# A mixer's output projection split into two passes over token halves, with the norms behind it overlapped

## The reference, cut to what matters

```python
def second_block(...):
    for l in range(DEPTH_2):                       # one layer
        mix = hybrid_mixer(rmsnorm(h, norm_mix_pre[l]), w_in[l], w_ret_out[l], w_sb_out[l], w_out[l])
        h = h + rmsnorm(mix, norm_mix_post[l])
        ff = swiglu(rmsnorm(h, norm_ffn_pre[l]), w_ffn_in[l], w_ffn_out[l])
        h = h + rmsnorm(ff, norm_ffn_post[l])
    return h[:, N_META:]

def hybrid_mixer(...):
    ...
    merged = jax.nn.sigmoid(ga) * y_ret + jax.nn.sigmoid(gb) * y_sb
    return merged @ w_out                          # the projection that is split

def rmsnorm(x, g):
    y = x * rsqrt(mean(x * x, axis=-1) + 1e-6)     # mean over the 1024 features of a token
    return y * g

def swiglu(hn, w_ffn_in, w_ffn_out):
    a, b = split(hn @ w_ffn_in, 2)
    return (silu(a) * b) @ w_ffn_out
```

## Time and profile before

| what | value |
|---|---|
| time of 3 runs, median | 2991.72 us (2991.7 to 2993.84) |
| the profiled execution | 2994.3 us, of which the profile spans 2992.6 |
| TensorE matmul busy | 2905.2 us (97%), 17931 matmuls |
| VectorE / ScalarE / GpSimd busy | 1464.2 / 1101.7 / 211.3 us |
| share of the chain that ended last | PE 62%, DVE 4%, ACT 1% |
| DMA | 225.63 MB, mean 75 GB/s |
| a weight load of 512 KB, issue to landing | 3.7 to 4.1 us (3.4 for 448 KB) |

### The profile page before, as it was taken

The page is one execution under the profiler, slowest core; times in us unless marked ns, Lnnn a source line. Parts: engine busy times, 40 slices in busy tenths (PEclk is TensorE's granted clock), DMA queues, the critical chain, the costliest instruction groups (busy, mean ns, idle before and its releaser), DMA issues.

```text
span 2992.6 us, 46575 instructions
## 1 busy us (share of the span) xinstructions
PE 2905.2 (97%) x17931; PEld 2517.2 (84%) x17931; DVE 1464.2 (49%) x2102; ACT 1101.7 (37%) x1763; POOL 211.3 (7%) x177
## 2 busy tenths in 40 slices
PE   8999999999989999799999999999999999799998
PEld 7878879999989999799988888888888887588887
DVE  5555545555347776555543454453433335544422
ACT  4333334333235554333322223223344444332322
POOL 1000001000011221100001011011000000200000
PEclk9999989999999999899999999999999999899999
DMA  4222213332331111133333322322311112133332
GB/s 126 55 53 60 62 30 92 91 90 85 91 105 57 49 56 44 53 94 91 91 91 99 95 67 87 89 68 74 88 45 54 42 54 78 58 98 95 92 91 73
DMA packets 419559, 225.63 MB, mean 75 GB/s; under 512 B 7589, under 2 KB 416422, under 8 KB 419350
## 3 DMA queue, kind: packets, MB, share of 16 engines
q1 hardware_dynamic: 416438, 211.45, 24.4%
q0 software_dynamic: 2256, 10.32, 1.2%
q10 hardware_dynamic: 784, 2.75, 0.3%
HBM read 222.36 MB, written 2.13 MB: 75 GB/s over the span
## 4 chain that ended last, share of the span: by engine, by line
PE 62%; DVE 4%; issue 2%; ACT 1%; POOL 0%; DVEq 0%; ACTq 0%; POOLq 0%
PE ps L436 33%; PE ps L440 17%; PE ps L1038 2%; PE ps L854 2%; PE ps L996 1%; PE ps L1059 1%; PE ps L1027 1%; DVE wl L403 1%; PE ps L963 1%; PE ps L899 1%; PE ps L1031 0%; DVE rl L2143 0%; DVE xl L470 0%; DVE post_t L518 0%; DVE h L521 0%
## 5 line engine op out<-in xcount | busy, mean ns | idle before, releaser
L403 DVE TENSOR_TENSOR wl<-raw,wh 128x1024 fp32r<-128x1024 f32 (+4 forms) x429 | 518.8, 1209 | 401.6 <-ACT wh L399 398.0
L399 ACT ACTIVATE wh<-raw 128x1024 fp32r<-128x1024 f32 (+4 forms) x429 | 428.5, 999 | 729.7 <-PE ps L436 394.1
L440 PE MATMUL ps<-xh,wh 128*128 128x264 f32 x2736 | 571.4, 290 | 14.4 <-DVE xl L470 5.5
L440 PE MATMUL ps<-xl,wh 128*128 128x264 f32 x2736 | 559.4, 286 | 0.0
L440 PE MATMUL ps<-xh,wl 128*128 128x264 f32 x2736 | 559.1, 286 | 0.0
L440 PEld LDWEIGHTS ps<-xh,wh 128*128 128x128 f32 x2736 | 429.6, 190 | 24.3 <-issue 7.4
L440 PEld LDWEIGHTS ps<-xl,wh 128*128 128x128 f32 x2736 | 427.2, 189 | 0.0
L440 PEld LDWEIGHTS ps<-xh,wl 128*128 128x128 f32 x2736 | 425.9, 190 | 0.0
L436 PE MATMUL ps<-xh,wh 128*128 128x512 f32 x976 | 391.6, 401 | 17.7 <-DVE xl L470 14.0
L436 PE MATMUL ps<-xl,wh 128*128 128x512 f32 x976 | 387.8, 397 | 0.0
L436 PE MATMUL ps<-xh,wl 128*128 128x512 f32 x976 | 385.6, 395 | 0.0
(11 more groups left out here) (309 smaller groups left out, 4011.4 us busy)
## 6 DMA issues: line engine op xcount, KB each, us to landing
raw<-in_w_in SPq DMA_DIRECT2D x88, 512.0 KB, 4.0
raw<-in_ffn_w_gate SPq DMA_DIRECT2D x44, 512.0 KB, 3.8
raw<-in_ffn_w_up SPq DMA_DIRECT2D x44, 512.0 KB, 3.8
raw<-in_w_ffn_in SPq DMA_DIRECT2D x44, 512.0 KB, 3.8
raw<-in_fox_w_in SPq DMA_DIRECT2D x33, 512.0 KB, 4.1
raw<-in_hgrn_w_in SPq DMA_DIRECT2D x32, 512.0 KB, 3.9
raw<-in_ffn_w_down SPq DMA_DIRECT2D x32, 448.0 KB, 3.4
raw<-in_ffn_w_down SPq DMA_DIRECT2D x16, 512.0 KB, 3.7
```

What stands on the lines that cost most here:

```text
L399: nc.scalar.activation(wh[:, v % 2, 0:nk, :], raw[:, v % RAW_SLOTS, 0:nk, :], ACT.Copy).then_inc(s("w_hi"), 1)
L403: nc.vector.tensor_tensor(wl[:, v % 2, 0:nk, :], raw[:, v % RAW_SLOTS, 0:nk, :], wh[:, v % 2, 0:nk, :].bitcast(F32), ALU.subtract).then_in ...
L440: last = nc.tensor.matmul(ps[:, bank + b, 0:HALF], w[:, slot, kk, :], x[:, k0 + k, b * HALF:(b + 1) * HALF], start=first, stop=end_)
```

## The change

PH_OUT now makes 256 tokens only (HALF_A), in 8 groups of 24 matmuls of 256 columns; a new phase PH_OUTB does the other 256 (HALF_B) with the same weights, which are loaded and split a second time. Norm, residual and xh, xl of the first half are placed in the steps of the second pass; of tiles 6 and 7 behind it. The first two groups of PH_UP2 are taken together: both over the first 256 tokens, then step by step over the second 256 as its norm goes on. Sums, rstd and squares are done in halves (SQUARES is the order of the squares). Elsewhere some semaphores are merged (p_inv and gate_one to fox_step, h_kept and ff_kept to kept, h_turned and ff_turned to turned), with the same instructions waiting for the same things.

```diff
-PH_UP2 = Phase(PH_OUT, FT // 2, K8, narrow=range(4))
+PH_OUTB = Phase(PH_OUT, 2, K8, narrow=range(4))
+PH_UP2 = Phase(PH_OUTB, FT // 2, K8, narrow=range(4))
...
+HALF_A, HALF_B = (0, SEQ // 2), (SEQ // 2, SEQ)
+SQUARES = [("mix", HALF_A, m) for m in range(KT)] + [("mix", HALF_B, 0), ("mix", HALF_B, 1)]
+for _m in range(2, KT):
+    SQUARES += [("h", HALF_A, _m - 2), ("mix", HALF_B, _m)]
+SQUARES += [("h", HALF_A, KT - 2), ("h", HALF_A, KT - 1)] + [("h", HALF_B, m) for m in range(KT)]
...
-    def post_norm(dve, src, post_row, r, n0, name, rx, next_row):
+    def post_norm(dve, part, m, r, n):
+        t0, t1 = META + part[0], META + part[1]
         dve.wait_ge(s("rstd_ready"), r + 1)
...                                               # post_t, h over t0:t1, as before
+        if m:
+            dve_x(dve, 5 + n // KT, m - 1, ROW_FFNPRE, t0, t1)
...
+        dense(PH_OUTB, dram["w_out_2"][0], 0)
...
TensorE:
-        dense(PH_OUT, mh, ml, ("m_ready", 0))
-        pe_sum(pe, 5, META)
-        dense(PH_UP2, xh, xl, ("x_ready", KT * 5), 6, META)
+        for m in range(KT):
+            pe_group(pe, PH_OUT, m // 4, m % 4, mh, ml, None if m else ("m_ready", 0), tokens=HALF_A)
+        for m in range(KT):
+            pe_group(pe, PH_OUTB, m // 4, m % 4, mh, ml, tokens=HALF_B)
+            if m == 0:
+                half_sum("mix", HALF_A).then_inc(s("ssum"), 1)
...
+        for gj in range(2):
+            pe.wait_ge(s("psum_free"), PH_UP2.g0 + gj + 1)
+            pe.wait_ge(s("w_split"), unit(PH_UP2, 0, gj) + RAW_SLOTS + 1)
+            for k in range(KT):
+                if gj == 0:
+                    pe.wait_ge(s("x_ready"), KT * 5 + k + 1)
+                up_step(gj, HALF_A, k)
+            if gj == 0:
+                half_sum("mix", HALF_B).then_inc(s("ssum"), 1)
+        for k in range(KT):
+            pe.wait_ge(s("x_ready"), KT * 6 + k + 1)
+            for gj in range(2):
+                last = up_step(gj, HALF_B, k)
+                if k == KT - 1:
+                    last.then_inc(s("mm_done"), 1)
+        half_sum("h", HALF_A)
+        half_sum("h", HALF_B).then_inc(s("ssum"), 1)
+        for gj in range(2, 4):
+            pe_group(pe, PH_UP2, 0, gj, xh, xl)
...
ScalarE:
+        for m in range(KT):
+            split_ahead(act, act_hi, PH_OUT, m // 4, m % 4)
+            if m == 4:
+                tables_for(act, "ln_exp")
+            act.wait_ge(s("psum_free"), evacuated(PH_OUT, m // 4, m % 4))
+            half_square("mix", HALF_A, m)
+        for m in range(KT):
+            split_ahead(act, act_hi, PH_OUTB, m // 4, m % 4)
+            if m >= 2:
+                half_x(HALF_A, m - 2)
+            act.wait_ge(s("psum_free"), evacuated(PH_OUTB, m // 4, m % 4))
+            half_square("mix", HALF_B, m)
+            if m == 0:
+                half_rstd(HALF_A, 5)
+        split_ahead(act, act_hi, PH_UP2, 0, 0)
+        half_x(HALF_A, KT - 2)
+        half_x(HALF_A, KT - 1)
+        half_rstd(HALF_B, 6)
+        for m in range(KT):
+            half_x(HALF_B, m)
+        up(2, PH_UP2, 7)
...
VectorE:
+        for m in range(KT):
+            mixed(PH_OUT, m, HALF_A)
+        for m in range(KT):
+            mixed(PH_OUTB, m, HALF_B)
+            if m >= 2:
+                post_norm(dve, HALF_A, m - 2, 5, m - 2)
+        split_ahead(dve, dve_lo, PH_UP2, 0, 0)
+        for m in range(KT - 2, KT):
+            post_norm(dve, HALF_A, m, 5, m)
+        dve_x(dve, 5, KT - 1, ROW_FFNPRE, META, META + HALF_A[1])
+        for m in range(KT):
+            post_norm(dve, HALF_B, m, 6, KT + m)
+        dve_x(dve, 6, KT - 1, ROW_FFNPRE, META + HALF_B[0], L)
+        up(2, PH_UP2, 7)
```

More of the change, by code:

```diff
@@ L413, in group_end, with pe_group @@
         return 2 + unit(ph, i, sum(map(len, ph.groups[:gj + 1])))
-    def pe_group(pe, ph, i, gj, hi, lo, ready=None, k0=0, part=None):
+    def pe_group(pe, ph, i, gj, hi, lo, ready=None, k0=0, part=None, tokens=(0, SEQ)):
         bank = ph.banks[(ph.g0 + gj) % 2]
@@ L435, in pe_group @@
                     if gj in ph.narrow:
-                        last = nc.tensor.matmul(ps[:, bank, 0:SEQ], w[:, slot, kk, :], x[:, k0 + k, META:L],
+                        last = nc.tensor.matmul(ps[:, bank, tokens[0]:tokens[1]], w[:, slot, kk, :],
+                                                x[:, k0 + k, META + tokens[0]:META + tokens[1]],
                                                 start=first, stop=end_)
@@ L511, in dve_add_h @@
         nc.vector.tensor_tensor(hm, hm, out_of(ph, mm), ALU.add).then_inc(s("psum_free"), 1)
-    def post_norm(dve, src, post_row, r, n0, name, rx, next_row):
+    def post_norm(dve, part, m, r, n):
+        t0, t1 = META + part[0], META + part[1]
         dve.wait_ge(s("rstd_ready"), r + 1)
[L516 to L524, removed]
+        nc.vector.scalar_tensor_tensor(post_t[:, m % 2, t0:t1], mix[:, m, t0:t1], col(gains, ROW_MIXPOST + m),
+                                       rstd[:, t0:t1], ALU.mult, ALU.mult).then_inc(s("post_scaled"), 1)
+        dve.wait_ge(s("post_scaled"), n + 1)
+        nc.vector.tensor_tensor(h[:, m, t0:t1], h[:, m, t0:t1], post_t[:, m % 2, t0:t1], ALU.add)\
+            .then_inc(s("h_post"), 1)
+        if m:
+            dve_x(dve, 5 + n // KT, m - 1, ROW_FFNPRE, t0, t1)
     def hgrn_level(n):
@@ L1099, in _, with half_sum, up_step, up_body @@
         dense(PH_SBOUT, oh, ol, ("sb_o_done", 1))
-        dense(PH_OUT, mh, ml, ("m_ready", 0))
-        pe_sum(pe, 5, META)
-        dense(PH_UP2, xh, xl, ("x_ready", KT * 5), 6, META)
+        def half_sum(what, part):
+            t0, t1 = META + part[0], META + part[1]
+            pe.wait_ge(s("sq_used"), square_index(what, part, KT - 1) + 3)
+            return nc.tensor.matmul(ps[:, 4, part[0]:part[1]], mean_d, ssq[:, t0:t1], start=True, stop=True)
+        for m in range(KT):
[4 more added lines that the diff above has]
+                half_sum("mix", HALF_A).then_inc(s("ssum"), 1)
+        def up_step(gj, part, k):
+            bank, slot = PH_UP2.banks[(PH_UP2.g0 + gj) % 2], (PH_UP2.u0 + gj) % 2
+            for n, (w, x) in enumerate(((wh, xh), (wh, xl), (wl, xh))):
+                last = nc.tensor.matmul(ps[:, bank, part[0]:part[1]], w[:, slot, k, :], x[:, k, META + part[0]:META + part[1]],
+                                        start=(k + n == 0), stop=(k == KT - 1 and n == 2))
+            return last
+        for gj in range(2):
[17 more added lines that the diff above has]
+            pe_group(pe, PH_UP2, 0, gj, xh, xl)
+        def up_body(i):
+            for gj in range(4):
+                pe_group(pe, PH_UP2, i, gj, xh, xl)
+        loop(pe, PH_UP2.n, up_body, 1)
         def turned_out(src, c, g, bank):
@@ L1131, in _ @@
                 mean.then_inc(s("ssum"), 1)
-        last.then_inc(s("ff_turned"), 1)
+        last.then_inc(s("turned"), 1)
     @block.scalar
```

122 lines of the change are left out of this document (70 added, 52 removed).

## The result

| | time, median | ratio to before, 95% interval | span of the profiled run |
|---|---|---|---|
| before | 2991.71 us (2991.58 to 2994.73, 6 runs) | | 2992.6 |
| the changed kernel | 3004.61 us (3003.47 to 3005.44, 6 runs) | 1.0041 (1.0030 to 1.0051) | 3003.7 |

The change made the kernel slower by 12.9 us, where 9.3 were forecast. So all traces are compared from the projection's first matmul on. From there to the end of the span before took 456.3 us, and the changed kernel 468.7: +12.4.

The account below looks back on a forecast made before the run. The prediction took TensorE to bound the projection, with 2 us a group to spare. Passes +13.0, stretch to the third feed-forward group -5.4 and clock +1.7 made +9.3 us: 3001 us forecast, range 2989 to 3009.

Parts of the forecast that it names:

- second pass: Projection's second 256 tokens: rounds of 4.58 us from the third group on, 31.4 us in all.
- last group's end to third feed-forward group: Stretch behind the projection: 31.8 us against 37.2 before, so -5.4 us.
- third group at half speed: Third feed-forward group's start: TensorE's clock falls in the lull ahead of it, +1.7 us.
- The order of the instructions makes the second pass slow: Second pass: ScalarE's high part stands behind work waiting for VectorE's h, so a round takes 4.58 us.
- GpSimd's additions hold nobody in the second pass: Second pass: half additions, some 0.7 us each, two a round, lie in the high part's time.
- Waits on raw: Both passes: the extra 4 MB of weight loads stay hidden; such waits would show that they don't.
- The tail: Behind the last projection group: 11.5 us through Ln and Exp, then eight second-half tiles on VectorE, 13.0 us.
- half sum and its wait 1.0: Behind the last projection group, ahead of Ln and Exp: the half sum with its wait takes 1.0 us.
- rival (a): TensorE's clock falls inside the second pass and the tail: +15 us, 3007 us; chance 0.12.
- An uncovered rstd, table and split: Ahead of the third feed-forward group: sums, Ln, Exp, table load and weight split with nothing beside them, 6.1 us.
- (b): Second pass: its round doesn't bind and TensorE sets the pace, +1.5 us, 2993 us; chance 0.17.
- (c): Passes at TensorE's pace, tail without collisions, no clock fall, shorter VectorE halves: -6.8 us, 2985 us; chance 0.11.

Follow-up runs that it names:

- lag_one: The changed kernel with ScalarE's xh and square of h of the first half one step later in the second pass; ratio to before 1.0014.
- passes_only: The kernel before with two passes of half the tokens and nothing else, the norm as a whole behind them; ratio to before 1.0020.
- no_h_adds: The changed kernel without GpSimd's seven additions of squares of h of the first half; ratio to before 1.0035.
- early: The changed kernel with the third feed-forward unit's split ahead of the second rstd and silu table, and of VectorE's first evacuation; ratio to before 1.0033.
- lag_early: The changed kernel with the changes of lag_one and early together; ratio to before 1.0008.
- unpair: The changed kernel with the second halves of the first two feed-forward groups made one behind the other; ratio to before 1.0050.

## Why the prediction was right

The direction, the mechanism and most of the size came out. By its own steps (trace against trace):

| step | forecast | measured |
|---|---|---|
| first pass | 26.25 us | 26.7 |
| second pass | 31.4 (round 4.58) | 32.5 (round 4.80) |
| both against one | +13.0 | +14.5 |
| last group's end to third feed-forward group | 31.8 | 33.3 |
| against 37.2 | -5.4 | -3.9 |
| third group at half speed | +1.7 | +1.75 |
| sum | +9.3 | +12.4 |

The traces' ends differ by the same 12.4, the timed medians by 12.9. No large errors cancel: the sum is 3.1 us short, about half of it in the passes and half behind them.

- *The order of the instructions makes the second pass slow.* Right, and shown by an intervention: lag_one changes the order alone and takes 7.4 us off up to the last copy. passes_only shows that the doubled weight work gives 7 of the 16 us by which the last copy comes later, and not most of them.
- *GpSimd's additions hold nobody in the second pass.* Wrong. They cost 0.25 us a round, as the low part's 1.48 shows beside 1.23 without them (no_h_adds). The prediction gave this as the upper bound of that term (0.3 a round).
- *Waits on raw.* Right: none. Each high part of this stretch starts right behind ScalarE's work ahead of it, or when TensorE is done with a group.
- *The tail.* The chain up to xl of tile 7 was forecast as 9.5 us and took 9.4; the eight tiles 13.0, and took 13.0 (the product written there, 1.6 x 8, is 12.8). The term that failed is "half sum and its wait 1.0". It took 2.5, since the clock had fallen by then: six matmuls in 1.65 us and a half sum of 0.87. By the rows at 2619.84 both together would take 1.3 at full speed, so that the clock makes 1.2 of the 1.5 us. The forecast sum had a clock fall only behind the norm; a fall in the tail stood in rival (a) alone.
- *An uncovered rstd, table and split.* Right: forecast 6.1, and 6.0 us lie between the last pair and the third group. early starts that group 1.9 us sooner, and then the first table load is in the way.
- *Rival (a), the clock falls inside the second pass and the tail.* In the tail it happened, and cost the 1.2 us above. In the second pass it happened once in the changed kernel, for one group and without cost, and in every second round of no_h_adds, with cost. Why it falls in one round and not in the next, these traces don't show. The Trainium skill ("TensorE: Matmul & The Clock Gate", "A second HAM failure mode: psum-queue depth-cycling") reports that short idling between groups of matmuls made the clock swing in another kernel. no_h_adds agrees: its clock went 0.93, 0.65, 1.00, 0.71 in successive stretches.
- *Rivals (b) and (c)*, that the round doesn't bind, are refuted by the rounds of 4.80.

Not settled: how much of the 12.9 us the fall of the clock before 2602 causes by itself. The 1.2 us are read from durations; no run held the clock up in that place alone.

## What to carry to other kernels

Where an engine's program alternates the splitting of the next weights with other work, one instruction that waits for a fresh result of another engine puts the whole round trip between the two into the pace of the matmuls; give it the result of the step before, which is there already. Before overlapping a serial stretch, see what its durations are made of: here 6.5 of 22.4 us went from VectorE's chain with GpSimd's additions, and moving these to TensorE, partly idle at that time, brought 7 to 9 us, where the best form of the overlap tried here (lag_early) brought none. Whether the overlap would pay with the sums on TensorE wasn't run. And count what two merged groups leave behind them with no matmul beside it, with the half-speed start that the lull brings.

## What the runs showed of the hardware that I had not expected

- A lull of TensorE of 5.2 us cost twice, by its length and by 1.75 us at half speed behind it; 20 unused matmuls in it took 1.6 us off in the trace.
- Fewer matmuls a step delayed what follows the norm (unpair, +2.7 us): the clock went from 1.00 to 0.80 in 4 us with 1.64 us of work and on to 0.50, while in the changed kernel it stayed at 1.00 with 0.97 to 1.25 us of work in every 2.
- VectorE and GpSimd hold each other up in work on 256 columns as on 512: an h of 0.42 us became 0.98 beside an addition of 0.73 (at 2609.9 of the changed kernel), and of 512 columns 0.69 became 1.82 beside one of 1.28 (at 2594.0 of before).
- The part of the program ahead of the change, the same in all kernels, took 2532.75 to 2536.30 us in the profiled executions. Against effects of a few us, only a comparison from a common point on tells them apart.
